# Low parts of the even u tiles made by an accumulating transfer, and twice as many fetched slots in the routing

## The reference

```
def peer_ffn(h, w_query, sub_keys, expert_u, expert_v):
    qry = (h @ w_query).reshape(T, P_HEADS, 2, P_HALF)
    scores = jnp.einsum("thcd,hcnd->thcn", qry, sub_keys)
    ...
    gates = jax.nn.softmax(best_s, axis=-1)
    def block(args):
        hb, eb, gb = args
        act = jax.nn.gelu(jnp.einsum("td,thkd->thk", hb, expert_u[eb]), approximate=False)
        return jnp.einsum("thk,thkd->td", act * gb, expert_v[eb])
```

## Time and profile before

| what | value |
|---|---|
| time, median of 3 runs | 1995.24 us (1991.93 to 1995.54) |
| span of the profiled execution | 1990.5 us |
| time of the profiled execution itself | not given; the median lies 4.7 us above its span |
| TensorE busy | 1935.9 us (97%) |
| VectorE busy | 1497.9 us (75%) |
| ScalarE busy | 723.5 us (36%) |
| u loop, v loop | from 822.9 us, from 1460.3 us |

### The profile page before, as it was taken

The page is one execution under the profiler, slowest core; times in us unless marked ns, Lnnn a source line. Parts: engine busy times, 40 slices in busy tenths (PEclk is TensorE's granted clock), DMA queues, the critical chain, the costliest instruction groups (busy, mean ns, idle before and its releaser), DMA issues.

```text
span 1990.5 us, 27945 instructions
## 1 busy us (share of the span) xinstructions
PE 1935.9 (97%) x10357; PEld 1710.3 (86%) x10357; DVE 1497.9 (75%) x2735; ACT 723.5 (36%) x1331; POOL 420.1 (21%) x231
## 2 busy tenths in 40 slices
PE   7999999999999999999999999999999999999998
PEld 4789777889877988999999999999988888888887
DVE  4776645364576537788889999996688898889986
ACT  4110233010351343343443444444444444444443
POOL 0333211444102023001111511111221222222210
PEclk9999999999999999999999999999999999999999
DMA  7235311353112432257668688888999999999993
GB/s 276 86 115 195 121 56 40 130 200 117 63 43 85 149 106 85 95 171 273 226 217 276 221 319 303 300 304 299 397 387 401 401 400 401 399 401 395 402 378 131
DMA packets 212644, 465.94 MB, mean 234 GB/s; under 512 B 15625, under 2 KB 157121, under 8 KB 193345
## 3 DMA queue, kind: packets, MB, share of 16 engines
q1 hardware_dynamic: 193408, 330.43, 47.7%
q0 software_dynamic: 18432, 134.23, 17.1%
q10 hardware_dynamic: 704, 0.04, 0.0%
HBM read 410.12 MB, written 54.53 MB: 233 GB/s over the span
## 4 chain that ended last, share of the span: by engine, by line
PE 43%; DMA 9%; DVE 4%; ACT 1%; issue 1%; SPq 1%; DVEq 0%; POOLq 0%; POOL 0%; ACTq 0%
PE xin_ps_u L2148 22%; PE xin_out L2192 16%; DMA experts_hot<-act_scratch 6%; PE xin_out L2170 4%; DMA con_raw<-in_expert_u 2%; DMA con_raw<-in_expert_v 1%; DVE over_v_vlo L2453 1%; DVE in_ulo L2304 1%; DVE experts_acc L1960 1%; SPq L2120 1%; DVE experts_rows L1941 1%; DVE xin_wt L2450 0%; ACT in_uhi L2221 0%; DVE xin_wlo L2455 0%; ACT L2263 0%
## 5 line engine op out<-in xcount | busy, mean ns | idle before, releaser
L1934 POOL DMA_INDIRECT experts_rows<-in_expert_rows,experts_idx x128 | 204.7, 1599 | 915.7 <-DVE experts_acc L1960 779.3
L2148 PE MATMUL xin_ps_u<-con_h_hi,in_uhi 128*128 128x384 f32 x1024 | 349.0, 341 | 11.3 <-DVE in_ulo L2304 9.1
L2148 PE MATMUL xin_ps_u<-con_h_hi,in_ulo 128*128 128x384 f32 x1024 | 343.3, 335 | 0.0
L2148 PE MATMUL xin_ps_u<-con_h_lo,in_uhi 128*128 128x384 f32 x1024 | 343.2, 335 | 0.0
L2192 PE MATMUL xin_out<-over_v_vhi,xin_whi 128*128 128x512 f32 x768 | 238.7, 389 | 2.3 <-DVE xin_wlo L2455 2.2
L2192 PE MATMUL xin_out<-over_v_vhi,xin_wlo 128*128 128x512 f32 x768 | 238.5, 389 | 0.0
L2192 PE MATMUL xin_out<-over_v_vlo,xin_whi 128*128 128x512 f32 x768 | 238.4, 389 | 0.0
L2304 DVE TENSOR_TENSOR in_ulo<-con_raw,in_uhi 128x1024 fp32r<-128x1024 f32 x127 | 155.2, 1222 | 81.2 <-ACT in_uhi L2221 78.7
L2148 PEld LDWEIGHTS xin_ps_u<-con_h_hi,in_uhi 128*128 128x128 f32 x1024 | 193.2, 189 | 15.6 <-DVE in_ulo L2304 13.0
L2148 PEld LDWEIGHTS xin_ps_u<-con_h_lo,in_uhi 128*128 128x128 f32 x1024 | 193.3, 189 | 0.0
L2148 PEld LDWEIGHTS xin_ps_u<-con_h_hi,in_ulo 128*128 128x128 f32 x1024 | 192.9, 188 | 0.0
(11 more groups left out here) (445 smaller groups left out, 3738.5 us busy)
## 6 DMA issues: line engine op xcount, KB each, us to landing
con_raw<-in_expert_u SPq DMA_DIRECT2D x128, 512.0 KB, 4.7
con_raw<-in_expert_v SPq DMA_DIRECT2D x128, 512.0 KB, 11.9
con_raw<-in_w_in SPq DMA_DIRECT2D x36, 1024.0 KB, 6.2
act_scratch<-in_act SPq DMA_DIRECT2D x128, 192.0 KB, 2.2
experts_hot<-act_scratch SPq DMA_DIRECT2D x128, 192.0 KB, 12.1
gate_scratch<-in_stage SPq DMA_DIRECT2D x12, 1024.0 KB, 7.2
gate_scratch<-over_s_stage SPq DMA_DIRECT2D x12, 1024.0 KB, 8.0
experts_hot<-gate_scratch SPq DMA_DIRECT2D x16, 768.0 KB, 14.0
```

The source lines that it names most:

```text
L1934: pool.indirect_dma_start(out=self.rows[:, r % ROWS, :], out_offset=None, in_=table, in_offset=at).then_inc(self.row_in[r % ROWS], 16)
L2148: mm = pe.matmul(ps_u[s % 2][:, 0:TD], a[s % 2][:, k, :], m[:, k, P:T], start=(i == 0), stop=(i == 3 * KD - 1))
```

## The change

For the even tiles 2, 4 ... 58 (LOW_BY_DMA, 29 tiles) VectorE no longer makes the low part. ScalarE writes the negated, rounded high part into `ulo`, then the high part into `uhi` as before. GpSimd issues a transfer of the same 512 KB of `expert_u` from memory, which adds onto `ulo`: -high + u is the low part. TensorE takes the 16 products with `uhi` of such a tile first and the 8 with `ulo` last, and waits for the transfer (`low_in`) between them. SP may reload a raw tile when both activations have read it. The table of slots gives the routing steps from 24 on a slot at every second step, and no longer at every fourth: 59 slots lie in the u loop and 69 in the v loop, where there were 51 and 77. GpSimd's fetches now stand between the accumulating transfers, each at a step given by FETCH_AT.

```diff
--- before.py
+++ after.py
@@ -1978,7 +1978,7 @@
     inside = [[] for n in range(NEXP)]
     r = 0
     for n in range(N_SEARCH + R_STEPS + 4, NEXP):
-        if (n < N_ROUTE and n % 4 == 0) or N_ROUTE <= n < N_HOT0 or (N_HOT0 <= n < N_HOT0 + N_HOT and n % 2 == 0) or (n >= N_HOT0 + N_HOT and n % 4 != 3):
+        if (n < N_ROUTE and n % 2 == 0) or N_ROUTE <= n < N_HOT0 or (N_HOT0 <= n < N_HOT0 + N_HOT and n % 2 == 0) or (n >= N_HOT0 + N_HOT and n % 4 != 3):
             inside[n].append(r)
             r += 1
     outside = [[] for n in range(NEXP)]
@@ -1993,6 +1993,19 @@
 
 IN_AT, OUT_AT = slots_of_steps()
 RING = U_RING
+WORKED_AT = [n for n in range(NEXP) for e in IN_AT[n]] + [NEXP + n for n in range(NEXP) for e in OUT_AT[n]]
+FETCH_AT = [N_SEARCH + R_STEPS] * ROWS + [n + 1 for n in WORKED_AT[:-ROWS]]
+LOW_BY_DMA = [n for n in range(NEXP) if n % 2 == 0 and 2 <= n < N_HOT0]
+
+
+def lows_by_dve(n):
+
+    return sum(m not in LOW_BY_DMA for m in range(n + 1))
+
+
+def lows_by_dma(n):
+
+    return sum(m in LOW_BY_DMA for m in range(n + 1))
 
 
 G_RUN = 4 * 8 * G_TOK
@@ -2059,14 +2072,23 @@
         block = al.block()
         assert N_TAIL > 0 and N_TAIL % 4 == 0
         STAGES, RANKS = 10, 9
+        neg_done, low_in = al.sem("neg_done"), [al.sem(f"low_in{i}") for i in range(2)]
         closed, summed = al.sem("closed"), al.sem("summed")
 
         @block.sync
         def _(sp):
+            def raw_tile_free(n):
+
+                if n in LOW_BY_DMA:
+                    sp.wait_ge(neg_done, lows_by_dma(n))
+                    sp.wait_ge(hi_done, n + 1)
+                else:
+                    sp.wait_ge(lo_done, lows_by_dve(n))
+
             def every(n):
                 if n >= 4:
 
-                    sp.wait_ge(lo_done, n - 3)
+                    raw_tile_free(n - 4)
                     sp.dma_start(raw[n % U_RING], u[n * P:(n + 1) * P, :]).then_inc(landed[n % U_RING], 16)
 
                     sp.wait_ge(gelu_done, n - 3)
@@ -2139,15 +2161,23 @@
         @block.tensor
         def _(pe):
             def every(n, s):
-                pe.wait_ge(lo_done, n + 1)
+                by_dma = n in LOW_BY_DMA if isinstance(n, int) else False
+                if by_dma:
+                    pe.wait_ge(hi_done, n + 1)
+                else:
+                    pe.wait_ge(lo_done, n + 1 - len(LOW_BY_DMA) if not isinstance(n, int) else lows_by_dve(n))
 
                 wait(pe, gelu_done, n - 1)
-                i = 0
-                for k in range(KD):
-                    for a, m in ((uhi, hT[0]), (uhi, hT[1]), (ulo, hT[0])):
-                        mm = pe.matmul(ps_u[s % 2][:, 0:TD], a[s % 2][:, k, :], m[:, k, P:T], start=(i == 0),
-                                       stop=(i == 3 * KD - 1))
-                        i += 1
+                parts = lambda some: [(k, a, m) for k in range(KD) for a, m in some]
+                if by_dma:
+                    todo = parts(((uhi, hT[0]), (uhi, hT[1]))) + parts(((ulo, hT[0]),))
+                else:
+                    todo = parts(((uhi, hT[0]), (uhi, hT[1]), (ulo, hT[0])))
+                for i, (k, a, m) in enumerate(todo):
+                    if by_dma and i == 2 * KD:
+                        pe.wait_ge(low_in[n % 2], 16 * sum(m % 2 == n % 2 and m <= n for m in LOW_BY_DMA))
+                    mm = pe.matmul(ps_u[s % 2][:, 0:TD], a[s % 2][:, k, :], m[:, k, P:T], start=(i == 0),
+                                   stop=(i == 3 * KD - 1))
                 mm.then_inc(u_done, 1)
 
             def turn_slots(tt):
@@ -2218,6 +2248,8 @@
                 act.wait_ge(landed[n % U_RING], 16 * (n // U_RING + 1))
 
                 wait(act, u_done, n - 1)
+                if n in LOW_BY_DMA:
+                    act.activation(ulo[n % 2][:], cut_of[n % U_RING], ACT.Copy, scale=-1.0).then_inc(neg_done, 1)
                 act.activation(uhi[n % 2][:], cut_of[n % U_RING], ACT.Copy).then_inc(hi_done, 1)
 
             def rounded(n):
@@ -2281,11 +2313,19 @@
 
         @block.gpsimd
         def _(pool):
-            pool.wait_ge(got.idx_done, 1)
-            for r in range(ROWS):
-                got.fetch(pool, r, A["expert_rows"])
-            for r in range(ROWS, SLOTS):
-                got.fetch(pool, r, A["expert_rows"])
+            e = 0
+            for n in range(NEXP):
+                if n + 1 in LOW_BY_DMA:
+                    pool.wait_ge(neg_done, lows_by_dma(n + 1))
+                    pool.dma_start(ulo[(n + 1) % 2][:], u[(n + 1) * P:(n + 2) * P, :].rearrange("p (k n) -> p k n", k=KD),
+                                   accum_op=ALU.add).then_inc(low_in[(n + 1) % 2], 16)
+                while e < SLOTS and n > FETCH_AT[e]:
+                    if e == 0:
+                        pool.wait_ge(got.idx_done, 1)
+                    got.fetch(pool, e, A["expert_rows"])
+                    e += 1
+            for e in range(e, SLOTS):
+                got.fetch(pool, e, A["expert_rows"])
             pool.wait_ge(ms0_done, 1)
             pool.tensor_tensor(rstd0[:], ms0[:], con.pow_half[:, 0:1], ALU.pow).then_inc(pow0_done, 1)
             def power(t):
@@ -2300,6 +2340,8 @@
         def _(dve):
             def cut(n):
 
+                if n in LOW_BY_DMA:
+                    return
                 dve.wait_ge(hi_done, n + 1)
                 dve.tensor_tensor(ulo[n % 2][:], cut_of[n % U_RING], as_f32(uhi[n % 2][:]), ALU.subtract).then_inc(lo_done, 1)
 
```

## The result

The changed kernel takes 2077.97 us (median of 4 runs, 2075.96 to 2080.0), the kernel before 1993.59 us (4 runs in the same session, 1990.92 to 1995.54): a ratio of 1.0422, 95% interval 1.0408 to 1.0435. It is slower by 84 us, where +27 was forecast with 2062 us as the upper end. The profiled execution has a span of 2075.2 us, before 1990.5.

The account below looks back on a forecast made before the run. TensorE, busy 97% of 1990.5 us, bounds the kernel. Lateness of 3.3 + 6 + 22.1 less 4.9 for VectorE gives +26.5, 2017; with 4.7 outside the span 2022 us, range 1990 to 2062.

Parts of the forecast that it names:

- the price of the adding transfer: Low part of even u tiles: issue to landing 5.2 us quiet, midway between 3.8 (plain load) and 6.5 (1 MB fetch).
- 31.4 us of lateness: TensorE's waits for the transfers in the u loop: 3.3 for tiles 2 to 22, 6 for tile 24, 22.1 for 26 to 58.
- The quiet term: Tiles 2 to 22, before fetches: each of 11 transfers lands 0.3 us late, 3.3 us in all.
- no visible extra: Issuing the transfer from GpSimd (POOL) instead of SP adds nothing visible to its landing time.
- Beside fetches: Tiles 26 to 58: 1.0 us added, landing after 6.2 us, 1.3 us late, 22.1 us for 17 tiles.
- The limit of 4.9 us: Even u tiles: time from transfer issue to needed landing; every us more costs one us of TensorE time.
- The burst of four fetches: First four fetches, queued behind tile 22's transfer, end about 931.0 us and make tile 24's transfer 6 us late.
- Rival 3: Adding transfer takes as long as a fetch, 6.5 us quiet, 7.5 beside fetches: +63, 2058 us; chance 0.18.
- VectorE's relief: Routing: 4.9 us lost to late VectorE; better spacing alone gains 2 us, but the sum took the full -4.9.
- The granted clock: TensorE's clock, 1.00 in the routing stretch, might fall with the new waits; that would come on top, unsized.
- Outside the span: Time beyond the profiled span: 4.7 us, the median run of 1995.24 less the span of 1990.5.

Follow-up runs that it names:

- the kernel with the third buffer: Changed kernel with a third buffer for low parts, so ScalarE negates and GpSimd issues the transfer one tile earlier: 2007.65 us, ratio 1.0073.
- loads held back: Changed kernel, with SyncE's u load and what stands behind it waiting until the adding transfer has landed: 2054.34 us, ratio 1.0317.
- third buffer, fetches apart: Changed kernel with a third buffer for low parts and the first four fetches issued one by one, two steps apart: 2001.32 us, ratio 1.0042.
- The kernel with filler products: Changed kernel with twelve products of unused result ahead of each TensorE wait for the adding transfer: 2075.81 us, ratio 1.0412.
- low parts alone: Changed kernel with the routing's slots back at every fourth step, the 29 adding transfers kept: 2072.67 us, ratio 1.0384.
- slots alone: Changed kernel with no adding transfer, VectorE making all low parts, routing slots kept at every second step: 1999.42 us, ratio 1.0033.

## Why the prediction was wrong

**The step that failed is the price of the adding transfer**: "I take (3.8 + 6.5)/2 = 5.2 us, that is 0.3 us late", and with it the 6.2 us beside fetches. Measured: 7.5 us in both stretches, 2.6 us late. The form of the sum held. The prediction had 31.4 us of lateness in it (3.3 + 6 + 22.1). With the measured landings, 219.8 us for the 29 transfers against 29 x 4.85, it is 79 us. The fallen clock adds 9.5 us, and VectorE's waits that are gone take off 4.2 us as the products show them, 7.4 as the weight loads do: 81 to 85 us, against a routing that is 82.3 us longer. The quiet term was mis-sized by a factor of nine (2.6 for 0.3), though its duration was off by 2.3 us of 5.2: near a limit the lateness is what counts.

**Why 7.5 and not 5.2** has three parts, and the runs do not part them cleanly. First, the plain copy itself: issued by GpSimd it takes 4.9 us in the quiet stretch, where SyncE's loads take 3.8, and 3.9 beside it in the same kernel. The prediction read "no visible extra" out of a slope between three rows, and missed these 1.1 us. They need not be the issuer: in the kernel with the third buffer two plain transfers that start over 2 us behind the last load, at 825.59 and 877.79 us, land after 4.1 us. Second, the addition: at the place where the changed kernel issues it, 7.5 us against 4.9. Third, company: the u load and the activation write start within 1.2 us ahead of it on the same engines, for they are set off by the same event (the end of the tile before). Where the loads are farther off, the adding transfer takes 6.0 us (loads held back) or 5.7 (third buffer, fetches apart), and there the addition is worth only 0.8 us (5.7 against 4.9). So addition and company cost more together than each alone. The engines' time per byte doubles, and the landing by itself does not. All this holds to some tenths: the kernels with the third buffer, with the fetches together and apart, do the same work up to 905 us, and have 6.5 and 5.7 us there. The prediction took the landing from rows of the quiet stretch as if a transfer stood alone there, and put contention only where fetches run.

**Beside fetches** the prediction added 1.0 us. Measured: none for the adding transfer in the changed kernel (7.5 quiet, 7.4 later, in the median), and 7.4 with half the fetches. The plain one does slow down, from 4.9 to 5.9. That the adding transfer shows nothing may come from the slower pace, which thins out the traffic (249 GB/s in that stretch); with the third buffer, at full pace and 0.98 to 0.99 engine share, the adding transfers took 7.6 to 8.3 us in the median against 5.7 to 6.5. So at full pace there is such a surcharge.

**What held.** The limit of 4.9 us from issue to landing (4.83 to 4.85 measured). The place and form of the wait: 28 waits for the transfer into in_ulo, the longest, 8.0 us, at tile 24. The burst of four fetches: 6 us predicted as tile 24's lateness and 8.2 measured, of which 2.6 are the ordinary lateness and 5.6 the burst. Of TensorE time in the v loop no more than about 1 us was won (below). Rival 3, twice the bytes, had 6.5 and 7.5 us with 2058 us, and was the nearest.

**VectorE's relief** was reckoned at 2 us by itself and then put into the sum with the full 4.9, on the ground that VectorE catches up while TensorE waits. That held: in the routing of the changed kernel TensorE waits for no low part of VectorE's. With the transfer plain and early, the one case in which the new path costs next to nothing, 3.9 of the 7.4 us at the weight loads remain, 1.3 us go to a late transfer, and the routing is 1.7 us shorter. So the smaller figure was right for that case.

**The granted clock** fell from 1.00 to 0.94 and 0.91, as the prediction feared, and the cost does come "on top": 9.5 us in the last eight products of the tiles, a term that the sum did not have. The kernel with filler products has the clock back; in its profile the landings are 7 us longer in all, which takes the gain away again.

**Outside the span** the prediction put 4.7 us. In every run of which both are on record the time is 1.7 to 2.0 us above the span; the rest of the 4.7 was the difference between one execution and the median of three. This moved the forecast by 3 us.

**A term that was missing: the end.** The last instruction of GpSimd's block is a DRAIN. First its row in the kernel before (duration in ns three times, start in us), then the rows of line 96 in the changed one:

```profile
L96 POOLq DRAIN  x1: 2142/2142/2142, 1986.1 to 1986.1; - x1
```

```profile
L96 POOLq DRAIN  x1: 9487/9487/9487, 2065.5 to 2065.5; - x1
...
L96 SPq EVENT_SEMAPHORE  x1: 17/17/17, 2075.2 to 2075.2; - x1
```

9.49 us where it was 2.14, and the execution ends 0.2 us after it: 5.3 us more after the last product. Over the kernels it goes so (slots dense: at every second step of the routing; sparse: at every fourth):

| kernel | slots | low parts | first gate product | last product starts | DRAIN | span |
|---|---|---|---|---|---|---|
| before | sparse | VectorE | 1086.4 | 1984.53 | 2.14 | 1990.5 |
| changed | dense | adding | 1169.6 | 2063.96 | 9.49 | 2075.2 |
| plain transfer | dense | plain | 1112.1 | 2006.36 | 9.49 | 2017.6 |
| low parts alone | sparse | adding | 1163.9 | 2065.86 | 1.16 | 2071.9 |
| slots alone | dense | VectorE | 1094.6 | 1991.53 | 2.14 | 1997.5 |
| third buffer, fetches apart | dense | adding | 1099.0 | 1993.77 | 9.74 | 2005.3 |
| the same, old table | sparse | adding | 1090.5 | 1990.59 | 1.16 | 1996.6 |
| the same as two above, plain | dense | plain | 1084.7 | 1979.77 | 9.73 | 1991.3 |

It is long in every kernel that has both the transfers of low parts and the dense table, and in none that has one alone; the addition has no part in it. The number of GpSimd's transfers is the same with either table, and its last fetch is issued 68 us or more before the end in all of them. What the DRAIN waits for stays open.

The table seems to show a second missing term. From the first gate product to the last product the four kernels in it with the dense table and the transfers need 894 to 895 us, the kernel before 898.1, and those with the old table and the transfers 900 and 902. But the dense table alone has 896.9, and of the kernels left out of the table those with the filler and with the fetches apart, dense and adding, have 899.5 and 897.6. In the v loop by itself, from its first product to its last, the dense table has 523.4 to 524.5 us, the kernel before 524.2, the old table with the transfers 525 and 526. So the slots moved out of the v loop may be worth about 1 us there against the kernel before; more is not shown.

## What to carry to other kernels

Before a transfer is put on the path between two tiles, count the time from the event that permits its issue to the one that needs it, and look at what else that same event sets off: here the adding transfer landed after 7.5 us close behind a load and a write, and after 6.0 with the loads held back. When the limit lies between two priced bounds, the middle is no safe choice, for each us beyond it is paid at every tile; here a buffer more, which gave 8 us and not 4.9, was worth 70 us. Even with the fetches apart it did not pay: of the last 8 us, 6 went with the addition, whose bytes hold the DMA engines twice as long as copied ones. A wait can also cost more than its length, when the products behind it run at a lower clock. And read the last 15 us of a profile apart from the rest: an instruction that closes an engine's queue can take back what the loops have won.

## What the runs showed of the hardware that was not expected

- While nothing is fetched, an adding transfer of 512 KB from GpSimd's queue lands after 6.0 us in the median (5.5 to 6.6) with the 512 KB loads held back, and after 7.5 when such a load and a 192 KB write start 0.8 to 1.2 us ahead; one of 256 KB there after 4.7 (4.6 to 5.6); a plain one of 512 KB there after 4.9 (4.3 to 6.2).
- It takes 6.6% of the 16 engines' time in a 90 us window for each MB, a plain transfer 3.3% from SyncE's queue and 3.4% from GpSimd's.
- Its issue keeps GpSimd busy for 0.84 to 1.13 us; the plain one for 0.53 to 0.80.
- A granted clock of 0.94 and 0.91 in the stretches where TensorE waits for a transfer in every second tile, and of 0.50 in eight products right behind a wait of 2.77 us, which then take 2.94 us and not 1.69. The eight products behind a wait of 2.57 us took 1.69.
- GpSimd's closing DRAIN took 1.16, 2.14, 9.49 or 9.73 us, the last two only in kernels that have both the transfers of low parts and the dense table. The cause is open.
